# The opening of a transformer trunk on one core: input by two queues, one summation for its mean, pool bands by two engines into four banks, and matmuls on constants ahead of them

## The reference, cut to what matters

```python
def rms_norm(x, g):
    xf = x.astype(jnp.float32)
    y = xf * lax.rsqrt(jnp.mean(xf * xf, axis=-1, keepdims=True) + EPS)
    return (y * g.astype(jnp.float32)).astype(x.dtype)

def multiscale_pool_mixer(h, w_pool, scale):
    ...
    for g, w in enumerate(POOL_WINDOWS):          # (2, 4, 8, 16), 512 features each
        hg = hf[..., g * POOL_GROUP:(g + 1) * POOL_GROUP]
        cs = jnp.cumsum(hg, axis=1)
        lagged = jnp.pad(cs, ((0, 0), (w, 0), (0, 0)))[:, :s]
        groups.append((cs - lagged) / cnt - hg)
    pooled = jnp.stack(groups, axis=2).astype(h.dtype)
    y = jnp.einsum('bsgc,gce->bsge', pooled, w_pool).reshape(b, s, d)
    return y * scale
```

## Time and profile before

| | |
|---|---|
| time, median of 3 runs | 1815.71 us (1815.68 to 1815.96) |
| the profiled execution's own time | 1815.7 us |
| its span, first to last instruction | 1813.9 us |
| TensorE matmuls busy | 1791.3 us, 99% of the span |
| VectorE, ScalarE, GpSimd busy | 1434.3, 993.8, 12.9 us |
| mean granted TensorE clock | 0.999 |
| chain that ended last | PE 96%, DVE 2%, issue 1% |

### The profile page before, as it was taken

One profiled execution on the slowest core, in us unless ns is written; L12 is line 12 of the kernel. 1 busy time (PEld: TensorE's weight loads), 2 busy tenths in 40 slices (PEclk: granted clock), 3 DMA queues, 4 the chain that ended last, 5 costly groups with the idle time before them and its releaser, 6 DMA issues.

```text
span 1813.9 us, 23165 instructions
## 1 busy us (share of the span) xinstructions
PE 1791.3 (99%) x8173; PEld 1490.1 (82%) x8173; DVE 1434.3 (79%) x1472; ACT 993.8 (55%) x1097; POOL 12.9 (1%) x15
## 2 busy tenths in 40 slices
PE   6999999999999999999999999999999999999998
PEld 5888888888888888888888888888888888888886
DVE  6897979888888976755557777898888879797976
ACT  6665656564655564633435545664646555565643
POOL 0000000000000000000000000000000000000000
PEclk9999999999999999999999999999999999999999
DMA  9455656555647474565554446555647464645671
GB/s 317 154 173 198 224 184 220 199 201 179 237 156 255 141 255 140 186 191 190 188 193 148 139 155 219 158 202 195 210 162 253 156 239 139 231 169 203 216 249 69
DMA packets 178487, 348.78 MB, mean 192 GB/s; under 512 B 10642, under 2 KB 10852, under 8 KB 178020
## 3 DMA queue, kind: packets, MB, share of 16 engines
q1 hardware_dynamic: 177696, 345.88, 56.6%
q10 hardware_dynamic: 708, 1.81, 0.3%
HBM read 345.55 MB, written 2.10 MB: 192 GB/s over the span
## 4 chain that ended last, share of the span: by engine, by line
PE 96%; DVE 2%; issue 1%; ACT 0%; DMA 0%; POOL 0%; SPq 0%; DVEq 0%; POOLq 0%; ACTq 0%
PE bank L1405 24%; PE bank L1407 24%; PE bank L1406 24%; PE bank L1381 6%; PE bank L1379 6%; PE bank L1380 6%; PE bank L1431 1%; PE bank L1397 1%; DVE w_lo L858 1%; DMA h<-in_x 0%; PE bank L1683 0%; DVE b_lo L918 0%; DVE a_lo L921 0%; PE bank L1629 0%; DVE h L1006 0%
## 5 line engine op out<-in xcount | busy, mean ns | idle before, releaser
L1405 PE MATMUL bank<-w_hi,u_hi_a 128*128 128x512 f32 x896 | 348.7, 389 | 0.0
L1407 PE MATMUL bank<-w_hi,u_lo_a 128*128 128x512 f32 x896 | 348.6, 389 | 0.0
L1406 PE MATMUL bank<-w_lo,u_hi_a 128*128 128x512 f32 x896 | 348.6, 389 | 0.0
L1405 PE MATMUL bank<-w_hi,mix_hi 128*128 128x512 f32 x684 | 267.7, 391 | 0.2
L1406 PE MATMUL bank<-w_lo,mix_hi 128*128 128x512 f32 x684 | 266.2, 389 | 0.0
L1407 PE MATMUL bank<-w_hi,mix_lo 128*128 128x512 f32 x684 | 266.2, 389 | 0.0
L514 ACT ACTIVATE w_hi<-arena 128x2048 fp32r<-128x2048 f32 x100 | 191.6, 1916 | 128.5 <-PE bank L1407 99.9
L870 DVE TENSOR_TENSOR w_lo<-arena,w_hi 128x2048 fp32r<-128x2048 f32 x100 | 227.6, 2287 | 40.4 <-ACT w_hi L514 40.4
L526 ACT ACTIVATE w_hi<-raw 128x1024 fp32r<-128x1024 f32 x112 | 118.9, 1062 | 181.0 <-PE bank L1407 171.1
L507 ACT ACTIVATE w_hi<-raw 128x1024 fp32r<-128x1024 f32 x128 | 133.6, 1062 | 149.3 <-PE bank L1381 145.0
L858 DVE TENSOR_TENSOR w_lo<-raw,w_hi 128x1024 fp32r<-128x1024 f32 x128 | 153.4, 1221 | 73.3 <-ACT w_hi L507 72.8
(11 more groups left out here) (175 smaller groups left out, 2767.8 us busy)
## 6 DMA issues: line engine op xcount, KB each, us to landing
raw<-in_w_mlp_in SPq DMA_DIRECT2D x128, 512.0 KB, 4.7
arena<-in_w_mlp_in SPq DMA_DIRECT2D x128, 512.0 KB, 5.4
raw<-in_w_mlp_out SPq DMA_DIRECT2D x128, 512.0 KB, 6.2
arena<-in_w_mlp_out SPq DMA_DIRECT2D x128, 512.0 KB, 5.7
raw<-in_w_kv SPq DMA_DIRECT2D x64, 512.0 KB, 4.4
raw<-in_w_q SPq DMA_DIRECT2D x32, 512.0 KB, 4.6
raw<-in_w_o SPq DMA_DIRECT2D x32, 512.0 KB, 4.0
raw<-in_pool_w SPq DMA_DIRECT2D x8, 512.0 KB, 7.5
```

The lines of the kernel that those rows point to most:

```text
L1405: nc.tensor.matmul(bank[:], hi, w_hi[:, slot, kk, :], start=begin, stop=False)
L1406: nc.tensor.matmul(bank[:], hi, w_lo[:, slot, kk, :], start=False, stop=False)
L1407: return nc.tensor.matmul(bank[:], lo, w_hi[:, slot, kk, :], start=False, stop=end)
```

## The change

- x comes in six pieces: SP issues one of 512 KB and two of 256 KB, ACT the other three. ACT squares those that SP issued, DVE those that ACT issued. Each square already carries the factor 1/2048, GpSimd writes EPS in a fifth column of `x_ssq`, and one summation on DVE gives the mean.
- The identity and the gains (five small transfers) are issued by GpSimd.
- The band constants are cut to the columns that are used (544 KB in place of 768 KB). DVE scales the bands of the first token block, ACT those of the second, each first for group 0 and then for the other three.
- `pool_bands(n)` writes to `T` for even n and to `X` for odd n, so `pool_bands(1)` waits for no reader. It waits for the gains instead, which lie in `X[0]`.
- The eight pieces of pool weights go to eight places (`raw` and the second half buffer in `arena`), and SP issues them without a wait. The squares go elsewhere in `arena`, and the MLP's second unit waits for `lo_ready` 6 and 8.
- A group starts when the first half of its pooled tiles and of its weights is there (`pool_group`).
- TensorE first does 26 matmuls on a constant tile (`keep_busy`), whose results nobody reads.

```diff
-C_POOL_END = 4 * 384
+C_BAND = REACH + P
+C_POOL_END = NG * C_BAND
 DVE_PIECES = [(0, slice(0, D)), (1, slice(0, 640)), (1, slice(640, 1280))]
 ACT_PIECES = [(1, slice(1280, D))]
+
+
+X_SP = [(0, slice(0, 1024)), (1, slice(0, 512)), (1, slice(512, 1024))]
+X_ACT = [(0, slice(1024, D)), (1, slice(1024, 1536)), (1, slice(1536, D))]
...
-        squares = place(0, TB, D)
+        squares = place(BACK, TB, D)
         pool_keep = place(4096, C_POOL_END)
         scale_row = place(8192, D)
         scaled = place(BACK + 15360, TB, SW)
         gain_rows = place(BACK + 13824, P)
+        warm_tile = place(10240, P)
...
+        bands = pool_keep.rearrange("p (g s) -> p g s", s=C_BAND)
+
+        def pooled_bank(n, b):
+            return (T, X)[n % 2][b]
+
...
-            def load_strip(s, source, first=False, after_mlp=False):
+            def load_pool(source):
+
+                for n in range(HALVES):
+                    sp.dma_start(raw_half[n // RAW][:, n % RAW], source(n // 2, n % 2)).then_inc(raw_landed[n], 16)
+
+            def load_strip(s, source, after_mlp=False):
                 for n in range(HALVES):
                     if after_mlp and n < RAW:
                         sp.wait_ge(lo_ready, end_at(0) + HALVES + n // 2 * 2 + 2)
-                    elif not (first and n < RAW):
+                    else:
...
-                    in_unit(layer, 0, 0, 0, at - 2, at)
                     if layer == 0:
-                        sp.wait_ge(x_squared, 1)
-                        sp.wait_ge(ssq_done, 3)
+                        in_unit(layer, 0, 0, 0, 2, 4)
+                        in_unit(layer, 0, 1, 1, 6, 8)
                     else:
+                        in_unit(layer, 0, 0, 0, at - 2, at)
                         sp.wait_ge(o_done, 2 * PAIRS)
-                    in_unit(layer, 0, 1, 1, None, None)
+                        in_unit(layer, 0, 1, 1, None, None)
...
-            for i in range(2 * TB):
-                tb, cols = i // 2, slice(i % 2 * (D // 2), (i % 2 + 1) * (D // 2))
-                sp.dma_start(h[:, tb, cols], x[0, tb * P:(tb + 1) * P, cols]).then_inc(x_landed[i], 16)
+            for (tb, cols), landed in zip(X_SP, x_sp_landed):
+                sp.dma_start(h[:, tb, cols], x[0, tb * P:(tb + 1) * P, cols]).then_inc(landed, 16)
             sp.dma_start(pool_keep, pool_consts).then_inc(pool_landed, 16)
-            load_strip(S_POOL, lambda g, hf: pool_view[0, g][:, 2 * hf:2 * hf + 2, :], first=True)
+            load_pool(lambda g, hf: pool_view[0, g][:, 2 * hf:2 * hf + 2, :])
...
+            nc.gpsimd.memset(x_ssq[:, :, 0:4], 0.0).then_inc(sums_cleared, 1)
+            nc.gpsimd.memset(x_ssq[:, :, 4:5], EPS).then_inc(sums_cleared, 1)
             nc.gpsimd.memset(neg_half[:], -0.5).then_inc(half_set, 1)
+            pool.dma_start(keep[:, 0:P], keep_consts[:, 0:P]).then_inc(ident_landed, 16)
+            pool.dma_start(gain_rows[G_MIX:G_MIX + 32, :], mix_norm.rearrange("l (k p) -> (l k) p", p=P)).then_inc(gains_landed, 16)
+            pool.dma_start(gain_rows[G_MLP:G_MLP + 32, :], mlp_norm.rearrange("l (k p) -> (l k) p", p=P)).then_inc(gains_landed, 16)
+            pool.dma_start(gain_rows[G_KV:G_KV + 16, :], kv_norm.rearrange("(k p) -> k p", p=P)).then_inc(gains_landed, 16)
+            pool.dma_start(gain_rows[G_SUB:G_SUB + 2, :], subln.rearrange("l (k p) -> (l k) p", p=P)).then_inc(gains_landed, 16)
...
-            act.dma_start(keep[:, 0:P], keep_consts[:, 0:P]).then_inc(ident_landed, 16)
-            act.dma_start(gain_rows[G_MIX:G_MIX + 32, :], mix_norm.rearrange("l (k p) -> (l k) p", p=P)).then_inc(gains_landed, 16)
-            act.dma_start(gain_rows[G_MLP:G_MLP + 32, :], mlp_norm.rearrange("l (k p) -> (l k) p", p=P)).then_inc(gains_landed, 16)
-            act.dma_start(gain_rows[G_KV:G_KV + 16, :], kv_norm.rearrange("(k p) -> k p", p=P)).then_inc(gains_landed, 16)
-            act.dma_start(gain_rows[G_SUB:G_SUB + 2, :], subln.rearrange("l (k p) -> (l k) p", p=P)).then_inc(gains_landed, 16)
-
-            for i in range(3):
-                tb, cols = i // 2, slice(i % 2 * (D // 2), (i % 2 + 1) * (D // 2))
-                act.wait_ge(x_landed[i], 16)
-                nc.scalar.activation(squares[:, tb, cols], h[:, tb, cols], ACT.Square,
-                                     accum_out=ssq[:, 0, tb, i % 2:i % 2 + 1]).then_inc(ssq_done, 1)
+            for (tb, cols), landed in zip(X_ACT, x_act_landed):
+                act.dma_start(h[:, tb, cols], x[0, tb * P:(tb + 1) * P, cols]).then_inc(landed, 16)
+
+            act.wait_ge(sums_cleared, 2)
+            for i, (tb, cols) in enumerate(X_SP):
+                act.wait_ge(x_sp_landed[i], 16)
+                slot = 2 * (i // 2)
+                nc.scalar.activation(squares[:, tb, cols], h[:, tb, cols], ACT.Square, scale=D ** -0.5,
+                                     accum_out=x_ssq[:, tb, slot:slot + 1]).then_inc(x_act_squared, 1)
             def pool_split(n):
-                act.wait_ge(raw_landed[n % RAW], 16 * (n // RAW + 1))
-                nc.scalar.activation(w_hi[:, n], raw[:, n % RAW], ACT.Copy).then_inc(hi_ready, 1)
+                act.wait_ge(raw_landed[n], 16)
+                nc.scalar.activation(w_hi[:, n], raw_half[n // RAW][:, n % RAW], ACT.Copy).then_inc(hi_ready, 1)
             def pooled_to_hi(n, b):
                 act.wait_ge(band_done, 2 * n + b + 1)
                 for c in (2 * b, 2 * b + 1):
                     kt = 4 * n + c
-                    nc.scalar.activation(b_tile(kt)[0], T[b][:, (c % 2) * SEQ:(c % 2 + 1) * SEQ], ACT.Copy,
+                    nc.scalar.activation(b_tile(kt)[0], pooled_bank(n, b)[:, (c % 2) * SEQ:(c % 2 + 1) * SEQ], ACT.Copy,
                                          scale=gain[:, G_MIX + kt:G_MIX + kt + 1]).then_inc(pooled_hi, 1)
+            act.wait_ge(pool_landed, 16)
+            act.wait_ge(rms_done, 1)
+            for w in (slice(0, 1), slice(1, NG)):
+                nc.scalar.activation(bands[:, w, REACH:], bands[:, w, REACH:], ACT.Copy, scale=rms[:, 0, 1:2]).then_inc(band_second, 1)
...
-            dve.wait_ge(x_landed[3], 16)
-            nc.vector.tensor_tensor_reduce(squares[:, 1, D // 2:D], h[:, 1, D // 2:D], h[:, 1, D // 2:D], 1.0, 0.0, ALU.mult, ALU.add,
-                                           ssq[:, 0, 1, 1:2]).then_inc(x_squared, 1)
-            dve.wait_ge(x_squared, 1)
-            norm_mean(0)
+            nc.vector.memset(warm_tile, 1.0).then_inc(warm_set, 1)
+            dve.wait_ge(sums_cleared, 2)
+            for i, (tb, cols) in enumerate(X_ACT):
+                dve.wait_ge(x_act_landed[i], 16)
+                slot = 1 if i == 0 else 2 * i - 1
+                nc.vector.tensor_tensor_reduce(squares[:, tb, cols], h[:, tb, cols], h[:, tb, cols], 1.0 / D, 0.0, ALU.mult, ALU.add,
+                                               x_ssq[:, tb, slot:slot + 1]).then_inc(x_dve_squared, 1)
+            dve.wait_ge(x_dve_squared, len(X_ACT))
+            dve.wait_ge(x_act_squared, len(X_SP))
+            nc.vector.tensor_reduce(mean[:, 0, :], x_ssq[:], AX.X, ALU.add).then_inc(mean_done, 1)
+            dve.wait_ge(pool_landed, 16)
+            dve.wait_ge(rms_done, 1)
+            for w in (slice(0, 1), slice(1, NG)):
+                nc.vector.tensor_scalar(bands[:, w, 0:REACH], bands[:, w, 0:REACH], rms[:, 0, 0:1], None, ALU.mult).then_inc(band_first, 1)
             dve.wait_ge(gains_turned, 1)
             nc.vector.tensor_copy(gain[:], X[0][:, 0:G_ROWS]).then_inc(gains_ready, 1)
             dve.wait_ge(gains_ready, 1)
             nc.vector.tensor_scalar(sub_gain[:], gain[:, G_SUB:G_SUB + 2], 1.0 - LAM_INIT, None, ALU.mult).then_inc(gains_ready, 1)
-            dve.wait_ge(pool_landed, 16)
-            dve.wait_ge(rms_done, 1)
-            bands = pool_keep.rearrange("p (g s) -> p g s", s=384)
-            nc.vector.tensor_scalar(bands[:, :, 0:SEQ], bands[:, :, 0:SEQ], rms[:, 0, 0:1], None, ALU.mult).then_inc(band_scaled, 1)
-            nc.vector.tensor_scalar(bands[:, :, SEQ:384], bands[:, :, SEQ:384], rms[:, 0, 1:2], None, ALU.mult).then_inc(band_scaled, 1)
             def pool_split(n):
                 dve.wait_ge(hi_ready, n + 1)
-                nc.vector.tensor_tensor(w_lo[:, n], raw[:, n % RAW], w_hi[:, n].bitcast(F32), ALU.subtract).then_inc(lo_ready, 1)
+                nc.vector.tensor_tensor(w_lo[:, n], raw_half[n // RAW][:, n % RAW], w_hi[:, n].bitcast(F32), ALU.subtract).then_inc(lo_ready, 1)
...
+            def keep_busy(count):
+
+                for _ in range(count):
+                    nc.tensor.matmul(PAIR[0][0][:, 0:P], warm_tile, warm_tile, start=True, stop=True)
+
+            pe.wait_ge(warm_set, 1)
+            keep_busy(26)
             pe.wait_ge(ident_landed, 16)
             pe.wait_ge(gains_landed, 64)
             nc.tensor.transpose(X[0][:, 0:G_ROWS], gain_rows[0:G_ROWS, :], ident[0:G_ROWS, 0:G_ROWS]).then_inc(gains_turned, 1)
-            def bands(n):
+            def pool_bands(n):
```

(70 more changed lines are left out.)

8 lines of the change are left out of this document (4 added, 4 removed).

## The result

The changed kernel takes 1823.54 us (median of six runs, 1821.32 to 1827.99), the kernel before 1815.70 (six runs, 1815.48 to 1816.16). The ratio is 1.0047, with a 95% interval of 1.0037 to 1.0057: 7.8 us slower, where 4.6 us faster was forecast. The profiled execution took 1826.85 with a span of 1825.0, which is 11.1 above the 1813.9 of before.

The account below looks back on a forecast made before the run. TensorE, busy 99% of the span, was taken as the bound, so only its waits ahead of group 0 could give time. 4.7 us there less 0.1 at DVE gave 4.6, from 1815.7 to 1811.1 us; whole range 1810.3 to 1817.0.

Parts of the forecast that it names:

- The 26 matmuls themselves cost nothing either, if they end before 12.25: Opening, TensorE: constant matmuls end near 8.8, or 12.2 at the slow pace, hidden either way; cost nothing.
- From there the chain stays on TensorE: From group 0 at 20.69 through lot 0, TensorE leads, so time saved ahead of 20.69 counts in full.
- Slower: Outcome of a time measurably above the kernel before; needs T above 18; chance 0.04.
- the unforeseen: Causes not named in the prediction, sharing the 0.04 chance of a slower kernel.
- T: Opening: the end of GpSimd's power on the mean; forecast 11.8 against 12.25 before, worth 0.45 us.
- my bound of 9.8: Opening: latest landing allowed for x's last piece, expected at 9.5, 0.3 earlier than before; lower bound 9.0.
- ScalarE's table load behind the first piece of x: Opening: the 1.28 us load waits for x at about 6.9, ends at 8.2, making ACT's squares later.
- GpSimd not ready: Rival, opening: five transfers and an unseen step delay GpSimd's power past the mean; 1813.5 to 1818; chance 0.35.
- The fast pace: Rival, bands ahead of group 0: idle TensorE loses the fast pace, group 0 at 17.9; 1813.0; chance 0.15.
- Bands and banks: Bands start at T + 0.45; with four banks sixteen matmuls run without waits, group 0 at T + 4.2.
- What is late next: Group 2 wanted at 30.9, its h_added at 30.8, weights by 24.2; both just suffice, 0.1 us taken off.
- the 1.75 us in hand: DVE's margin at group 2 in the kernel before: 35.63 against h_added at 33.88; forecast to be used up.

Follow-up runs that it names:

- e5: The changed kernel without its 26 constant matmuls and the memset and wait that serve them; 1813.93 us, ratio 0.9990.
- e1: The kernel before with only the 26 constant matmuls (and the memset that feeds them) added; 1821.83 us, ratio 1.0036.
- e2: The kernel before with 42 constant matmuls added and nothing else of the change; 1815.91 us, ratio 1.0002.
- e3: The changed kernel with 41 constant matmuls in place of 26; 1812.78 us, ratio 0.9984.
- e7: The changed kernel with 22 constant matmuls in place of 26; 1816.73 us, ratio 1.0011.
- e9: On e6, all six pieces of x issued by SyncE's queue, ScalarE's and VectorE's in turn; 1813.38 us, ratio 0.9987.
- e12: On e6, x on one queue as in e9, plus another order of splits and first h_added on VectorE and ScalarE; 1812.96 us, ratio 0.9984.
- e6: The changed kernel with 11 constant matmuls of 512 columns in place of 26 of 128; 1812.80 us, ratio 0.9984.
- e4: The changed kernel with 20 constant matmuls in place of 26; 1814.88 us, ratio 1.0001.
- e8: On e6, the pooled bands written into two banks again in place of four; 1815.53 us, ratio 0.9998.

## Why the prediction was wrong

**The step that failed.** "The 26 matmuls themselves cost nothing either, if they end before 12.25", together with "From there the chain stays on TensorE" as the reason that only the stretch ahead of 20.69 counts. I priced the matmuls as work on an idle engine. They are also 104 instructions, and they move all TensorE's code behind them by 0.43 blocks of 16 KB. Both MLP loops then touch eight blocks, their code is fetched again in the second pass, and TensorE stalls four times and runs 3.4 us at half pace twice, 13.5 us by the profile. Against e5, the change without these matmuls, it is 9.6 by the medians. e1 shows it with the matmuls alone (6.1), e2 and e3 take it away by adding more, e7 does it for one loop. "Slower" stood at 0.04, by GpSimd and "the unforeseen"; none of the rivals was this.

**T.** Forecast 11.8, measured 12.17 against 12.25 before. x was mis-sized: the last piece landed at 10.39, not at 9.5, and beyond my bound of 9.8. Before, with four pieces and no transfers by GpSimd, it was 9.77. What made it later is open. The pool constants follow SyncE's pieces and could take bandwidth from x's last piece on the other queue, but with all of x on one queue ahead of them it still lands at 10.29 (e9) and 10.24 (e12). Between 6 and 7 us the DMA engines move 162 GB/s in the changed kernel, 255 in e9 and 379 before. ScalarE's table load behind the first piece of x came as forecast and did no harm, since VectorE was last.

**GpSimd not ready (0.35).** False. The five transfers ended at 4.11 and the power began with the mean. The Trainium skill (GPSIMD Engine Reference, Instruction dispatch) has about 6 us for a first call into fresh code; from 4.11 that would end at 10.1, an estimate, ahead of the mean at 11.3, so the trace neither shows it nor excludes it.

**The fast pace (rival, 0.15).** The rival came true in the changed kernel: 12.80 to 16.07 at the slow pace after 3.4 us with little work, group 0 at 18.08, forecast 17.9. It does hold in e3 and e6, where the constant matmuls run up to the bands: then the pace is 0.234 throughout. The Trainium skill (TensorE: Matmul & The Clock Gate, Part 1) says that idleness halves the clock and sustained work brings it back; the trace agrees, with 0.50 from 12.58 and 1.00 again from 15.99. (In the kernel before, the trace's clock begins at 17.91, so the 1.00 of the earlier trace rows says nothing of the slow stretch ahead of it.)

**Bands and banks.** Right: no gap between `pool_bands(0)` and `pool_bands(1)`, and 4.38 from T to group 0 in e3 against 4.2.

**What is late next.** Right in e3, at 32.2 for `h_added` where 30.8 was forecast. In the changed kernel itself TensorE reached group 2 only at 33.00 and had no wait. The last weight landed at 25.7, not 24.2. The margin was also misread: 14.94 from group 0 to group 2 and the 1.75 us in hand take one end from the timeline and the other from the chain, and by the timeline alone they are 14.70 and 1.51. With the code in place, the change is worth 2.9 us of the 4.6 forecast: 0.4 by T, 0.2 by the banks' stretch and some 1 us by `h` are missing. Another 0.3 goes in small steps between 60 and 1700 us in e3's profile, for which I have no cause.

**Shares.** Taken away one at a time: the four banks 2.7 us, the busy time ahead of the bands 1.1, weights without slots 0.9, the second queue 0.6. They add up to 5.3 and not to 2.9. The banks' 2.7 holds 1.7 of lost clock, and the last two move the same wait at group 2; that this is all of the difference is not shown.

**Still open.** The exact edge (a loop end between 43.023 and 43.055 blocks), why the cost of fetching again differs from run to run (1821.3 to 1828.0 in the changed kernel), and why it is smaller in e1.

## What to carry to other kernels

An instruction added ahead of a loop has a second price, where it pushes the loop's code. Compare the q8 row of the page before and after, and if it grew by more than the code did, look at the passes of the loops for waits on "issue". For work that shall only keep TensorE busy, take few wide matmuls and let them run right up to the real ones, but not past them (e12).

## What the runs showed of the hardware that I had not expected

- TensorE's loops of 6.3 blocks of 16 KB ran their second pass without a fetch when they lay in seven blocks (50 or 51 packets), and with nine packets per loop when in eight (59 for one, 68 for both). With only a few instructions in the eighth block (e4), the one profile had no fetch. A stall was 1.7 to 3.8 us long, by the starts of the matmuls around it.
- Behind the stalls in the changed kernel (from 353.91 and 1435.94) and the waits for a bank in e2 (from 20.13) and e8 (from 18.02), the granted clock was at its lower level for 3.41 us each time, which cost 1.7 us more. A single wait of 1.57 (e9, and e1 in layer 0) or of 1.43 (e7) cost only its length.
- A missing block of code can show in the profile as a wait for whichever engine finished last (e1, e7).
